# The last plain float32 product of a block-multiplied up projection, rewritten in three fp32r passes and dealt to other banks

## The chip, the cores and the metric

The kernel runs on one NeuronCore of one Trainium2 chip. The metric is the device time of one execution in microseconds, as the median of several runs. TensorE (PE) multiplies, VectorE (DVE), ScalarE (ACT) and GpSimd (POOL) work on vectors, and SyncE (SP) and GpSimd issue DMAs.

## The reference

One inference step of a one-layer decoder, all in float32, for 512 prompt tokens and 8 × 4 sample tokens (544 columns). The mixer in front is untouched. The part at hand is the convolutional feed-forward:

```python
u = h @ w_ffn_up                        # 1024 -> 2 x 2816: a gate half and a value half
ext = concatenate([conv_state, u], axis=1)
c = conv_b + sum(conv_w[i] * ext[:, i:i + T] for i in range(3))
g, val = c[..., :2816], c[..., 2816:]
f = (gelu(g) * val) @ w_ffn_down
```

## The kernel before

Activations lie transposed, features over the 128 partitions and the 544 tokens as columns. Each of the two halves of `u` has 22 tiles of 128 features. A float32 product is made as three passes in fp32r: weights and activations are each split into a high part (rounded by a copy on ScalarE) and a low part (the difference, on VectorE), and `high*high`, `high*low` and `low*high` are added up in a bank.

The first three pairs of tiles (gate tile n and value tile n) are multiplied plainly. From pair n = 3 (`NPLAIN`) to 21 a block scheme makes the four 2x2 blocks of (gate, value) x (tokens 0 to 271, tokens 272 to 543), each with 8 blocks of the contraction, from 7 products instead of 8. A product has 4 contraction blocks of 128 and 272 columns. Its weights are the gate weights (products 1 and 2), sums of weights "s13" (products 5 and 7) and "s24" (products 6 and 3), and, for product 4, the upper half of the value weights `v_high`. Its activations are halves of the hidden state (`T1h`, `T1l`) or the sums t1 to t4. Six products go in three fp32r passes (`three_passes`, lines 2245 to 2247, 12 matmuls each). Product 4 (line 2306) is 4 plain float32 matmuls on the raw `v_high` and `t4raw`; the profile records two matmuls for each.

TensorE's order for pair n, with what each waits for: 6 (s24 low part, `s1_ready`), 5, 7 (`q_ready`), 1 of pair n+1 (gate low part), 4 (`r_neg`), 3 (`u_two[1]`), 2 of pair n+1. Products 1, 6, 7 and 4 pile up in bank A, which ScalarE copies out after 1 (`keep_first`, line 1531), 6 (`keep_second`, 1537), 7 (`keep_third`, 1543) and 4 (`value_first`, 1550). Products 5 and 3 pile up in bank C, read on VectorE by `value_second` (2975 and 2976) and `gate_second` (2965 and 2966). Product 2 has bank 6 alone, read on VectorE by `gate_first` (2958).

The queues are written out by hand. In iteration n VectorE runs: `gate_second(n-1)`, `gate_first(n)`, the four taps of the convolution of pair n-1 (2849, 2855), `sum_2(n+1)` (2929), `sums_13_lo(n+1)` (2945), `value_second(n)`, `sum_4(n+1)` (2937), `f_product(n-1)` (2871), `gate_lo(n+2)` (2917), `sums_24_lo(n+1)` (2951). ScalarE runs: `first_tap(n-1, 0)` (1483), `keep_second(n)`, `sums_13_hi(n+1)` (1514), `keep_third(n)`, `gelu(n-1)` (1489), `gate_hi(n+2)` (1504), `keep_first(n+1)`, `sums_24_hi(n+1)` (1524), `value_first(n)`, `first_tap(n, 1)`.

SyncE loads the weights of later pairs: when product 2 of pair n is done the gate weights of pair n+2 (`load_g`, line 704, 512 KB), when product 7 is done the low value half of pair n+3 (711, 2 x 256 KB), when product 4 is done the high value half of pair n+2 (715, 256 KB), and right behind it one DMA that moves a piece of the attention cache from DRAM to DRAM (674, mostly 511 KB). GpSimd adds weights onto the landed low half by accumulating DMAs (993, 2 x 256 KB), and copies the heads and tails of the convolution (974, 983, 984).

After pair 21 comes the down projection (lines 1673 to 1675, sample tokens at 1692). Its operands `fTh` and `fTl` come from `f_high` (ScalarE) and `f_low` (VectorE), and those of the first four tiles are made while the last pair runs.

## Time and profile before

| What | Value |
|---|---|
| Time, median of 3 runs | 987.57 us (986.95 to 987.87) |
| The profiled execution's own time | 986.23 us |
| Its span, first to last instruction | 984.4 us |
| TensorE matmul busy | 960.6 us (98%) |
| VectorE, ScalarE, GpSimd busy | 600.7, 424.0, 276.2 us |
| Granted TensorE clock, mean | 0.999 |
| HBM traffic | 242 GB/s over the span |

The profile page splits the span by engine. Matmuls overlap (one starts before the one before it has drained), so the distance from start to start is what a matmul costs, not its duration. The trace can be asked for rows in order of time (start, length, engine, line, what is written and read, and in brackets the idle time ahead of it and what ended it), for groups by line, for waits, and for busy time in a stretch. The block scheme runs from about 628 to 838 us, the down projection behind it to the end.

### The profile page before, as it was taken

Reading aid. Unit: us, or ns where it says so; the run is one execution under the profiler, and the core shown is the slowest. Engines: PE = TensorE matmul, PEld = TensorE weight load, DVE = VectorE, ACT = ScalarE, POOL = GpSimd, SP = SyncE. Lnnn points to the kernel's source line nnn. Section 1 sums busy time; section 2 is a strip of 40 time slices with the busy share of each in tenths; the row PEclk is TensorE's granted clock in tenths of the full one; section 3 lists DMA queues with packets and bytes.
Section 4 is the critical chain, followed back from the end, with each engine's and each line's share of the span. In section 5 each row is a group of like instructions: output and inputs, shape, how many; then the busy total and the mean of one; then the engine's idle time right before and its main releaser. Section 6 shows DMA issues by size and latency. Waiting matters only on the chain. (4 is left out here: it accounts for less than half of the span.)

```text
span 984.4 us, 19132 instructions
## 1 busy us (share of the span) xinstructions
PE 960.6 (98%) x7470; PEld 845.5 (86%) x7470; DVE 600.7 (61%) x1030; ACT 424.0 (43%) x851; POOL 276.2 (28%) x412
## 2 busy tenths in 40 slices
PE   6999999999999999999999999999999999999997
PEld 4888787779999989999888788899999999777775
DVE  5455125436356887876127588798888888533235
ACT  5333323432543333333224366565566556433313
POOL 1102003144171344445201006235653650000200
PEclk9999999999999999999999999999999999999999
DMA  7534445555697677678834357678887882444853
GB/s 290 201 128 159 170 167 181 183 171 172 249 307 252 223 229 236 191 237 268 285 108 160 122 176 246 149 206 214 219 219 209 218 207 88 171 160 151 299 182 120
DMA packets 55750, 195.03 MB, mean 198 GB/s; under 512 B 8312, under 2 KB 14904, under 8 KB 54128
## 3 DMA queue, kind: packets, MB, share of 16 engines
q1 hardware_dynamic: 32336, 130.17, 39.0%
q0 software_dynamic: 23040, 63.07, 23.1%
q8 instruction: 59, 0.97, 0.4%
q10 hardware_dynamic: 288, 0.59, 0.2%
q14 instruction: 27, 0.22, 0.1%
HBM read 181.57 MB, written 56.27 MB: 242 GB/s over the span
## 5 line engine op out<-in xcount | busy, mean ns | idle before, releaser
L2370 DVE TENSOR_TENSOR wlo<-wraw,whi 128x1024 fp32r<-128x1024 f32 x94 | 114.8, 1221 | 258.9 <-ACT whi L1053 258.7
L1053 ACT ACTIVATE whi<-wraw 128x1024 fp32r<-128x1024 f32 x94 | 99.7, 1060 | 299.8 <-PE bank L1675 185.5
L1673 PE MATMUL bank<-whi,T1h 128*128 128x512 f32 (+1 forms) x288 | 113.5, 394 | 0.1
L1760 PE MATMUL bank<-T1h,whi 128*128 128x272 f32 x384 | 113.4, 295 | 0.0
L1766 PE MATMUL bank<-T1h,wlo 128*128 128x272 f32 x384 | 111.0, 289 | 0.0
L1765 PE MATMUL bank<-T1l,whi 128*128 128x272 f32 x384 | 110.4, 287 | 0.0
L1675 PE MATMUL bank<-whi,T1l 128*128 128x512 f32 (+1 forms) x288 | 109.9, 382 | 0.0
L1674 PE MATMUL bank<-wlo,T1h 128*128 128x512 f32 (+1 forms) x288 | 109.9, 381 | 0.0
L1760 PEld LDWEIGHTS bank<-T1h,whi 128*128 128x128 f32 x384 | 72.3, 188 | 4.8 <-issue 4.5
L1765 PEld LDWEIGHTS bank<-T1l,whi 128*128 128x128 f32 x384 | 72.4, 189 | 0.0
L1766 PEld LDWEIGHTS bank<-T1h,wlo 128*128 128x128 f32 x384 | 72.2, 188 | 0.0
L1673 PE MATMUL bank<-whi,fTh 128*128 128x512 f32 x176 | 71.4, 406 | 0.0
L1674 PE MATMUL bank<-wlo,fTh 128*128 128x512 f32 x176 | 69.5, 395 | 0.0
L1675 PE MATMUL bank<-whi,fTl 128*128 128x512 f32 x176 | 69.4, 394 | 0.0
L1673 PEld LDWEIGHTS bank<-whi,T1h 128*128 128x128 f32 x288 | 58.1, 202 | 12.7 <-issue 3.9
L1675 PEld LDWEIGHTS bank<-whi,T1l 128*128 128x128 f32 x288 | 58.1, 202 | 9.9
L1674 PEld LDWEIGHTS bank<-wlo,T1h 128*128 128x128 f32 x288 | 58.3, 202 | 8.8
L993 POOL DMA_DIRECT2D s_raw<-in_weights x38 | 37.5, 1209 | 77.6 <-DMA s_raw<-in_weights 77.5
L984 POOL COPY cv_tail<-u 128x16 f32<-128x16 f32 x44 | 54.2, 1569 | 0.0
L983 POOL COPY cv_tail<-u 128x2 f32<-128x2 f32 x44 | 43.5, 1241 | 27.1 <-ACT u L1550 22.4
L974 POOL COPY u<-cv_state 128x16 f32<-128x16 f32 x44 | 43.5, 1131 | 24.0 <-DVE c L2855 18.7
L2569 DVE TENSOR_TENSOR prod<-kvk,qbc 128x512 f32<-128x512 f32 x48 | 33.0, 687 | 23.7 <-DMA qbc<-sample_queries 22.8
(367 smaller groups left out, 2594.2 us busy)
## 6 DMA issues: line engine op xcount, KB each, us to landing
wraw<-in_weights SPq DMA_DIRECT2D x102, 512.0 KB, 4.4
out_s_kv_g<-in_cache_kv_g SPq DMA_DIRECT2D x64, 511.0 KB
qbc<-sample_queries POOLq DMA_DIRECT2D x48, 256.0 KB, 4.9
s_raw<-in_weights SPq DMA_DIRECT2D x38, 256.0 KB, 3.7
g_raw<-in_weights SPq DMA_DIRECT2D x19, 512.0 KB, 6.2
s_raw<-in_weights POOLq DMA_DIRECT2D x38, 256.0 KB, 7.1
kvk<-in_cache_kv_g POOLq DMA_DIRECT2D x32, 256.0 KB, 3.9
kvv<-in_cache_kv_g POOLq DMA_DIRECT2D x16, 512.0 KB, 8.4
```

Source lines behind the costliest of these rows:

```text
L974: nc.gpsimd.tensor_copy(u_samples(n, j)[:, :, 0:2], cvs[:, 16 * tile:16 * tile + 16].rearrange("p (b t) -> p b t", t=2)).then_inc(head_rea ...
L983: nc.gpsimd.tensor_copy(cvt[:, 18 * tile:18 * tile + 2], ubs[:, n % 3, j, SEQ:SEQ + 2])
L984: nc.gpsimd.tensor_copy(cvt[:, 18 * tile + 2:18 * tile + 18].rearrange("p (b t) -> p b t", t=2), u_samples(n, j)[:, :, 4:6]).then_inc(tail ...
L993: pool.dma_start(s13_raw[r][:, 2 * a_:2 * a_ + 2, :], src, accum_op=ALU.add).then_inc(sum_in[r], 16)
L1053: nc.scalar.activation(w_halves(s)[0], w_source(s), ACT.Copy).then_inc(w_hi, 1)
L1673: one = mm(P[i][:, 0:w], xh, Wh, start=st, stop=False)
L1674: mm(P[i][:, 0:w], xh, Wl, start=False, stop=False)
L1675: return one, mm(P[i][:, 0:w], xl, Wh, start=False, stop=sp_)
L1760: one = mm(dst, Wh, Th[:, k, c], start=k == 0, stop=False)
L1765: mm(dst, Wh, Tl[:, k, c], start=False, stop=False)
L1766: last = mm(dst, Wl, Th[:, k, c], start=False, stop=k == kt - 1)
L2370: v.tensor_tensor(lo, w_source(s), hi.bitcast(F), ALU.subtract).then_inc(w_lo, 1)
```

## The change

Product 4 goes through `three_passes` like the others. For that `v_high` is split on each pair by `value_hi` (ScalarE, 128x512) and `value_lo` (VectorE, 128x512), and t4 once by `operand_hi` and `operand_lo` (128x1088). The high part of `v_high` has a single buffer, so `value_hi(n)` waits for product 4 of the pair before. The high part of t4 lies where `fTl` of the first tiles is written later, so `f_low` of tiles 0 to 3 waits for the last product 4.

The products are dealt anew. Bank A gets 1, 6, 5, 3 and bank C gets 7, 4, and the order on TensorE is 6, 7, 5, 1 of n+1, 3, 4, 2 of n+1. So `keep_third` copies after product 5, `gate_second` moves to ScalarE (two copies out of bank A after product 3), and `value_first` moves to VectorE (after product 4). Wherever gate and value come in turn, the gate comes first: taps, GpSimd's heads and tails. On ScalarE `gelu(n-1)` goes ahead of `keep_third(n)`. Loads keep their rules, with the low value half now behind product 5 and the high value half still behind product 4, which is now the last but one in the order. The diff also renames semaphores (three into one, `s_soft`); those hunks, the `PRODUCT_NO[.., 7]` that become `[.., 5]` in ScalarE's waits, and the reorder ahead of the loop are left out below.

```diff
-        order += [(n, 6), (n, 5), (n, 7)] + [(n + 1, 1)] * nxt + [(n, 4), (n, 3)] + [(n + 1, 2)] * nxt
+        order += [(n, 6), (n, 7), (n, 5)] + [(n + 1, 1)] * nxt + [(n, 3), (n, 4)] + [(n + 1, 2)] * nxt
...
+    v_high_lo = [sb(f"v_high_lo{e}", VH_AT[e], [128, 512], R) for e in range(2)]
+    v_high_hi = sb("v_high_hi", 51752, [128, 512], R)
+    assert 51752 + 512 <= 52392
+    t4lo = sb("t4lo", TT0 + 6528, [128, 4, HALF], R)
+    t4hi = sb("t4hi", 4352, [128, 4, NTOK], R)[:, :, HALF:NTOK]
...
-        return 2 * n + 2 - j
+        return 2 * n + 1 + j
...
-            sp.wait_ge(product, PRODUCT_NO[n, 7])
+            sp.wait_ge(product, PRODUCT_NO[n, 5])
             if n + 3 < FT:
                 load_v_low(n + 3)
             sp.wait_ge(product, PRODUCT_NO[n, 4])
...
             act.wait_ge(t_raw, 2 + k)
+            if k == 4:
+                act.wait_ge(w_used, S_UP + 2 * NPLAIN)
             nc.scalar.activation(hi[:], raw[:], ACT.Copy).then_inc(t_hi, 1)
...
+        def value_hi(n):
+
+            e = pair_set(n)
+            act.wait_ge(vh_in[e], set_count(n))
+            if n > NPLAIN:
+                act.wait_ge(product, PRODUCT_NO[n - 1, 4])
+            nc.scalar.activation(v_high_hi[:], v_high[e][:], ACT.Copy).then_inc(vh_hi, 1)
+
...
-            act.wait_ge(product, PRODUCT_NO[n, 7])
+            act.wait_ge(product, PRODUCT_NO[n, 5])
             act.wait_ge(u_two[1], n)
-            nc.scalar.activation(rr[:], P[bank_a(n)][:, 0:HALF], ACT.Copy, scale=-1.0).then_inc(r_neg, 1)
-
-        def value_first(n):
-
-            act.wait_ge(product, PRODUCT_NO[n, 4])
-            act.wait_ge(conv_done, conv_no(n - 3, 1))
-            act.wait_ge(tail_done, conv_no(n - 3, 1))
-            nc.scalar.activation(ubs[:, n % 3, 1, 2:2 + HALF], P[bank_a(n)][:, 0:HALF], ACT.Copy, scale=-1.0).then_inc(u_one[1], 1)
+            nc.scalar.activation(rr[:], P[bank_a(n)][:, 0:HALF], ACT.Copy).then_inc(h_kept, 1)
+
+        def gate_second(n):
+
+            b = P[bank_a(n)]
+            act.wait_ge(product, PRODUCT_NO[n, 3])
+            act.wait_ge(conv_done, conv_no(n - 3, 0))
+            act.wait_ge(tail_done, conv_no(n - 3, 0))
+            nc.scalar.activation(ubs[:, n % 3, 0, 2 + HALF:2 + SEQ], b[:, 0:SEQ - HALF], ACT.Copy)
+            nc.scalar.activation(u_samples(n, 0)[:, :, 2:6], by_tokens(b[:, SEQ - HALF:HALF]), ACT.Copy).then_inc(u_two[0], 1)
...
         for n in range(NPLAIN, FT):
-            first_tap(n - 1, 0)
+            first_tap(n - 1, 1)
             keep_second(n)
+            if n == NPLAIN:
+                operand_hi(4, t4raw, t4hi)
+                value_hi(NPLAIN)
             if n + 1 < FT:
                 sums_13_hi(n + 1)
             else:
                 w_split(S_DN + 1)
                 f_high(2)
+            gelu(n - 1)
             keep_third(n)
-            gelu(n - 1)
...
-            value_first(n)
-            first_tap(n, 1)
-        first_tap(FT - 1, 0)
+            gate_second(n)
+            if n + 1 < FT:
+                value_hi(n + 1)
+            first_tap(n, 0)
+        first_tap(FT - 1, 1)
...
-        def product_5(n):
+        def product_7(n):
             e = pair_set(n)
             pe.wait_ge(s13_lo, pair_no(n))
-            pe.wait_ge(t_lo, 3)
             if n >= NPLAIN + 2:
-                pe.wait_ge(u_two[0], n - 1)
+                pe.wait_ge(u_one[1], n - 1)
             elif e:
                 pe.wait_ge(u_two[1], NPLAIN)
-            three_passes(P[bank_c(n)], True, *sums_13(n, 1), 0, lambda k: t1hi[:, k, :], lambda k: t1lo[:, k, :])
-
-        def product_7(n):
+            three_passes(P[bank_c(n)], True, *sums_13(n, 0), 0, lambda k: t3hi[:, k, :], lambda k: t3lo[:, k, :])
+
+        def product_5(n):
+
+            pe.wait_ge(q_ready, pair_no(n))
+            three_passes(P[bank_a(n)], False, *sums_13(n, 1), 0, lambda k: t1hi[:, k, :], lambda k: t1lo[:, k, :])
+
+        def product_4(n):
             e = pair_set(n)
-            pe.wait_ge(q_ready, pair_no(n))
-            three_passes(P[bank_a(n)], False, *sums_13(n, 0), 0, lambda k: t3hi[:, k, :], lambda k: t3lo[:, k, :])
-
-        def product_4(n):
+            pe.wait_ge(vh_lo, pair_no(n))
+            pe.wait_ge(t_lo, 4)
+            pe.wait_ge(u_two[1], n + 1)
+            three_passes(P[bank_c(n)], False, v_high_hi, v_high_lo[e], 0, lambda k: t4hi[:, k, :], lambda k: t4lo[:, k, :])
+
+        def product_3(n):
             e = pair_set(n)
-            pe.wait_ge(vh_in[e], set_count(n))
-            pe.wait_ge(t_raw, 6)
-            pe.wait_ge(r_neg, pair_no(n))
-            for k in range(4):
-                last = mm(P[bank_a(n)][:, 0:HALF], v_high[e][:, 128 * k:128 * k + 128], t4raw[:, k, :], start=False, stop=k == 3, skip_group_check=True)
-            last.then_inc(product, 1)
-
-        def product_3(n):
-
-            e = pair_set(n)
-            pe.wait_ge(u_two[1], n + 1)
-            three_passes(P[bank_c(n)], False, s24_high[e], s24_low[e], 512, lambda k: T1h[:, 4 + k, second_half], lambda k: T1l[:, 4 + k, second_half])
+            pe.wait_ge(h_kept, pair_no(n))
+            three_passes(P[bank_a(n)], False, s24_high[e], s24_low[e], 512, lambda k: T1h[:, 4 + k, second_half], lambda k: T1l[:, 4 + k, second_half])
         product_1(NPLAIN)
         product_2(NPLAIN)
         for n in range(NPLAIN, FT):
             product_6(n)
+            product_7(n)
             product_5(n)
-            product_7(n)
             if n + 1 < FT:
                 product_1(n + 1)
+            product_3(n)
             product_4(n)
-            product_3(n)
...
             dve.wait_ge(f_hi, n + 1)
+            if n < 4:
+                dve.wait_ge(product, PRODUCT_NO[FT - 1, 4])
...
+        def value_lo(n):
+
+            e = pair_set(n)
+            dve.wait_ge(vh_hi, pair_no(n))
+            dve.wait_ge(s24_made, 2 * pair_no(n) - 1)
+            v.tensor_tensor(v_high_lo[e][:], v_high[e][:], v_high_hi[:].bitcast(F), ALU.subtract).then_inc(vh_lo, 1)
...
-        def gate_second(n):
+        def value_first(n):
+
+            dve.wait_ge(product, PRODUCT_NO[n, 4])
+            dve.wait_ge(q_ready, pair_no(n))
+            v.scalar_tensor_tensor(ubs[:, n % 3, 1, 2:2 + HALF], P[bank_c(n)][:, 0:HALF], -1.0, qq[:], ALU.mult, ALU.subtract
+                                   ).then_inc(u_one[1], 1)
+
+        def value_second(n):
             b = P[bank_c(n)]
-            dve.wait_ge(product, PRODUCT_NO[n, 3])
-            dve.wait_ge(q_ready, pair_no(n))
-            v.tensor_tensor(ubs[:, n % 3, 0, 2 + HALF:2 + SEQ], b[:, 0:SEQ - HALF], qq[:, 0:SEQ - HALF], ALU.add)
-            v.tensor_tensor(u_samples(n, 0)[:, :, 2:6], by_tokens(b[:, SEQ - HALF:HALF]), by_tokens(qq[:, SEQ - HALF:HALF]), ALU.add
-                            ).then_inc(u_two[0], 1)
-
-        def value_second(n):
-
-            b = P[bank_c(n)]
-            dve.wait_ge(product, PRODUCT_NO[n, 5])
-            dve.wait_ge(r_neg, pair_no(n))
+            dve.wait_ge(product, PRODUCT_NO[n, 7])
+            dve.wait_ge(h_kept, pair_no(n))
             dve.wait_ge(tail_done, conv_no(n - 3, 1))
-            v.tensor_tensor(ubs[:, n % 3, 1, 2 + HALF:2 + SEQ], rr[:, 0:SEQ - HALF], b[:, 0:SEQ - HALF], ALU.subtract)
-            v.tensor_tensor(u_samples(n, 1)[:, :, 2:6], by_tokens(rr[:, SEQ - HALF:HALF]), by_tokens(b[:, SEQ - HALF:HALF]), ALU.subtract
-                            ).then_inc(u_two[1], 1)
+            v.scalar_tensor_tensor(ubs[:, n % 3, 1, 2 + HALF:2 + SEQ], b[:, 0:SEQ - HALF], -1.0, rr[:, 0:SEQ - HALF], ALU.mult, ALU.subtract)
+            v.scalar_tensor_tensor(u_samples(n, 1)[:, :, 2:6], by_tokens(b[:, SEQ - HALF:HALF]), -1.0, by_tokens(rr[:, SEQ - HALF:HALF]),
+                                   ALU.mult, ALU.subtract).then_inc(u_two[1], 1)
...
-                gate_second(n - 1)
+                value_first(n - 1)
             gate_first(n)
             conv(n - 1)
+            if n == NPLAIN:
+                operand_lo(4, t4raw, t4hi, t4lo)
+            value_lo(n)
             if n + 1 < FT:
                 sum_2(n + 1)
                 sums_13_lo(n + 1)
-            else:
-                f_low(0)
-                f_low(1)
             value_second(n)
...
-                f_low(2)
-                f_low(3)
-        gate_second(FT - 1)
+                for k in range(4):
+                    f_low(k)
+        value_first(FT - 1)
```

## Rows read from the trace of the kernel before

**Rows 1.** The page, first part: busy time, share, instructions.

```profile
PE 960.6 (98%) x7470; PEld 845.5 (86%) x7470; DVE 600.7 (61%) x1030; ACT 424.0 (43%) x851; POOL 276.2 (28%) x412
```

**Rows 2.** Busy time of the engines over 15 pairs, granted clock, DMA share.

```profile
643.76:807.35 163.59, 163.48 (x1202) 158.51 (x1202) 144.06 (x226) 99.78 (x151) 85.73 (x122) 1.00 0.84 214
```

**Rows 3.** Groups by line and shape, 600 to 860 us: busy, mean ns.

```profile
L2306 PE MATMUL bank<-t4raw,v_high 128*128 128x272 f32 x152 | 38.1, 393 | 1.9 <-ACT rr L1543 1.9
...
L2929 DVE TENSOR_TENSOR s_raw<-s_raw,v_high 128x512 f32<-128x512 f32 x19 | 13.0, 683 | 3.7 <-DMA s_raw<-in_weights 3.7
...
L2905 DVE SCALAR_TENSOR_TENSOR t4raw<-t2raw,x_sum 128x1088 f32<-128x1088 f32 x1 | 1.3, 1291 | 0.0
```

**Rows 4.** Timeline of TensorE through one pair: start, length, line.

```profile
730.66 0.28 PE L2245 MATMUL bank<-t2hi,s_high 128*128 128x272 f32 x1
...
735.16 0.29 PE L2245 MATMUL bank<-T1h,g_high 128*128 128x272 f32 x1
...
736.68 1.99 PE L2306 MATMUL bank<-t4raw,v_high 128*128 128x272 f32 x8
738.31 0.49 PE L2245 MATMUL bank<-T1h,s_high 128*128 128x272 f32 x1
738.63 0.29 PE L2246 MATMUL bank<-T1l,s_high 128*128 128x272 f32 x1
...
741.53 0.29 PE L2245 MATMUL bank<-t2hi,s_high 128*128 128x272 f32 x1
```

**Rows 5.** Timeline of VectorE through one pair that waited for nothing.

```profile
709.14 0.44 DVE L2958 TENSOR_TENSOR u<-bank,s 128x272 f32<-128x272 f32 x1 [0.73 <-PE bank L2247]
709.50 1.50 DVE L2849 SCALAR_TENSOR_TENSOR c<-u,convp,c 128x560 f32<-128x560 f32 x2
...
717.08 1.22 DVE L2951 TENSOR_TENSOR s_low<-s_raw,s_high 128x1024 fp32r<-128x1024 f32 x1
```

**Rows 6.** Timeline of all engines around one late load of gate weights.

```profile
738.70 0.33 SPq L715 DMA_DIRECT2D v_high<-in_weights  x1
739.07 0.52 SPq L674 DMA_DIRECT2D out_s_kv_g<-in_cache_kv_g  x1
...
740.05 1.77 POOL L993 DMA_DIRECT2D s_raw<-in_weights  x2 [3.93 <-DMA s_raw<-in_weights]
...
741.73 0.33 SPq L704 DMA_DIRECT2D g_raw<-in_weights  x1
...
746.53 0.66 ACT L1489 ACTIVATE c<-c 128x560 f32<-128x560 f32 x1
749.07 1.06 ACT L1504 ACTIVATE g_high<-g_raw 128x1024 fp32r<-128x1024 f32 x1 [1.88 <-DMA g_raw<-in_weights]
...
751.40 1.22 DVE L2951 TENSOR_TENSOR s_low<-s_raw,s_high 128x1024 fp32r<-128x1024 f32 x1
...
752.68 0.39 PE L2245 MATMUL bank<-t2hi,s_high 128*128 128x272 f32 x1
```

**Rows 7.** Waits between 640 and 820 us: total, times, longest.

```profile
ACT g_high L1504 <- DMA g_raw<-in_weights: 12.7, 11, 1.9
```

**Rows 8.** Timeline of ScalarE: the two other latest gate loads.

```profile
650.82 1.06 ACT L1504 ACTIVATE g_high<-g_raw 128x1024 fp32r<-128x1024 f32 x1 [1.57 <-DMA g_raw<-in_weights]
...
814.62 1.06 ACT L1504 ACTIVATE g_high<-g_raw 128x1024 fp32r<-128x1024 f32 x1 [1.81 <-DMA g_raw<-in_weights]
```

**Rows 9.** DMA share in 40 slices of 0.15 us, 738 to 744 us.

```profile
DMA  9984111100099369992999990002735996596567
```

**Rows 10.** Timeline at the first pair and behind the last one.

```profile
637.18 1.06 ACT L1514 ACTIVATE s_high<-s_raw 128x1024 fp32r<-128x1024 f32 x1 [3.99 <-DMA s_raw<-in_weights]
...
638.67 2.07 PE L2306 MATMUL bank<-t4raw,v_high 128*128 128x272 f32 x8 [1.36 <-ACT rr L1543]
...
838.35 1.08 PE L1692 MATMUL bank<-wraw,fTs 128*32 128x128 f32 x32 [0.30 <-PE bank L2247]
...
839.36 0.50 PE L1673 MATMUL bank<-whi,fTh 128*128 128x512 f32 x1
```

More of the change, by code:

```diff
@@ L512, in build_layer @@
     kw_in = [sem(f"kw_in{e}") for e in range(2)]
-    s_step, pads_ready, qbd_ready, v_used, s_probs = (sem("s_step"), sem("pads_ready"), sem("qbd_ready"),
-                                                     sem("v_used"), sem("s_probs"))
-    s_max, s_exp, o_row, os_hi, os_lo = (sem(n) for n in ("s_max", "s_exp", "o_row", "os_hi", "os_lo"))
+    s_step, pads_ready, qbd_ready, v_used, s_soft = (sem("s_step"), sem("pads_ready"), sem("qbd_ready"),
+                                                     sem("v_used"), sem("s_soft"))
+    o_row, os_hi, os_lo = (sem(n) for n in ("o_row", "os_hi", "os_lo"))
     branch_done = sem("branch_done")
@@ L526, in build_layer @@
     vl_in, sum_in = ([sem(f"{nm_}{e}") for e in range(3)] for nm_ in ("vl_in", "sum_in"))
-    g_hi, g_lo, s13_hi, s13_lo, s24_made, s24_hi, s24_lo = (
-        sem(nm_) for nm_ in ("g_hi", "g_lo", "s13_hi", "s13_lo", "s24_made", "s24_hi", "s24_lo"))
+    g_hi, g_lo, s13_hi, s13_lo, s24_made, s24_hi, s24_lo, vh_hi, vh_lo = (
+        sem(nm_) for nm_ in ("g_hi", "g_lo", "s13_hi", "s13_lo", "s24_made", "s24_hi", "s24_lo", "vh_hi", "vh_lo"))
     t_raw, t_hi, t_lo = sem("t_raw"), sem("t_hi"), sem("t_lo")
-    s1_ready, q_ready, r_neg = sem("s1_ready"), sem("q_ready"), sem("r_neg")
+    s1_ready, q_ready, h_kept = sem("s1_ready"), sem("q_ready"), sem("h_kept")
     x2_moved = sem("x2_moved")
@@ L968, in conv_heads @@
         def conv_heads(n):
-            for j in (1, 0):
+            for j in (0, 1):
                 tile = n + FT * j
@@ L977, in conv_tails @@
         def conv_tails(n):
-            for j in (1, 0):
+            for j in (0, 1):
                 tile = n + FT * j
@@ L1046, in w_split @@
             elif s == S_DN:
-                act.wait_ge(product, PRODUCT_NO[FT - 2, 7])
+                act.wait_ge(product, PRODUCT_NO[FT - 2, 5])
                 assert sum_set(FT - 3) == 1
@@ L1510, in sums_13_hi @@
             if n >= NPLAIN + 2:
-                act.wait_ge(product, PRODUCT_NO[n - 2, 7])
+                act.wait_ge(product, PRODUCT_NO[n - 2, 5])
             elif e:
@@ L1570, in _ @@
         w_split(S_UP + 3)
+        first_tap(0, 0)
         first_tap(0, 1)
-        first_tap(0, 0)
         operand_hi(1, t3raw, t3hi)
@@ L1582, in _ @@
         sums_13_hi(3)
+        first_tap(1, 0)
         first_tap(1, 1)
-        first_tap(1, 0)
         columns(2, 0)
@@ L1587, in _ @@
         gelu(1)
+        first_tap(2, 0)
         columns(2, 1)
-        first_tap(2, 1)
         keep_first(3)
@@ L1606, in _ @@
             else:
-                act.wait_ge(product, PRODUCT_NO[FT - 2, 7])
+                act.wait_ge(product, PRODUCT_NO[FT - 2, 5])
                 if n == FT - 2:
@@ L1996, in sample_turn @@
         def sample_turn():
-            pe.wait_ge(s_probs, 1)
+            pe.wait_ge(s_soft, 3)
             turn(("sp",), [srow[:, g, 0:128] for g in range(NG)], 128)
@@ L2261, in product_1 @@
             if n >= NPLAIN + 2:
-                pe.wait_ge(u_one[1], n - 1)
+                pe.wait_ge(u_two[0], n - 1)
             elif e:
@@ L2858, in conv @@
         def conv(n):
+            second_tap(n, 0)
             second_tap(n, 1)
-            second_tap(n, 0)
+            third_tap(n, 0)
             third_tap(n, 1)
-            third_tap(n, 0)
         def f_product(n):
```

18 lines of the change are left out of this document (9 added, 9 removed).

## The prediction

> **What bounds the kernel now.** I read the page first: matmuls fill 98% of the span [rows 1]. Then the stretch of 15 pairs from one gate load to the fifteenth after it: 163.59 us, so 10.91 us a pair. TensorE is busy in 163.48 of it at full clock, VectorE in 144.06 (9.60 a pair), ScalarE in 99.78 (6.65) [rows 2]. So TensorE sets the pace here, and VectorE is the next in line with 1.3 us to spare. The groups and TensorE's timeline then say what a product costs [rows 3, 4], VectorE's timeline how long its chain is [rows 5], and the rows around a late load what happens when weights come late [rows 6 to 8]: that is the one other thing that reaches TensorE in this stretch.
>
> **Product 4 itself.** Products 6, 5 and 7 take from 730.66 to 735.16: 1.50 us each, 125 ns a matmul. The float32 product starts at 736.68, the next one at 738.31, and that one's second matmul comes 0.32 later instead of 0.125. So product 4 costs 1.63 + 0.195 = 1.825 us [rows 4]. In three passes it is a product like the others, same shape and same kind of operands: 1.50. Gain 0.325 a pair, times 19 pairs: 6.2 us. The pair's period without waits goes from 10.87 (730.66 to 741.53) to about 10.53.
>
> The Trainium skill (FP8 and Floating Point Precision, TensorE Precision Notes) says that true float32 takes four passes through the array. By that the product would be 16 passes against 12 and each pair would gain 0.50, 9.5 us in all. The trace puts it at 1.825 us, 14.6 passes of 125 ns, and the trace decides.
>
> **VectorE.** With no wait, its chain from `gate_first` to the end of `sums_24_lo` takes 709.14 to 718.30, 9.16 us [rows 5]. The change adds `value_lo`, 0.68 long and about 0.60 from start to start, since neighbours overlap by some 0.08 [rows 3]. `gate_second` goes, and `value_first` comes in its place in front of `gate_first`, as long as `gate_first`, 0.36 from start to start (709.14 to 709.50) [rows 5]. Subtractions become scalar_tensor_tensor with an immediate, whose row (1291 ns for 1088 columns) shows no markedly dearer rate than 683 ns for 512 [rows 3]; I count 0.02. The cycle is then 9.16 - 0.08 + 0.60 + 0.36 + 0.02 = 10.06 us against 10.53. Priced from below at nothing for the new form and from above at 0.1 for each of the three, it stays between 10.04 and 10.36: hidden, with 0.2 to 0.5 to spare. If that cover were gone, each 0.1 over would cost 1.8 us over 18 pairs.
>
> **ScalarE.** It gains `value_hi` (1024 columns take 1.06 [rows 10], so 512 about 0.6) and two copies for one; 6.65 becomes some 7.5 of 10.53, hidden. `value_hi(n+1)` waits for product 4 of n, which ends 9.2 us into the pair, and holds up only `first_tap(n, 0)` behind it, which then ends about at the start of the next pair; VectorE reads it 0.6 us later. Two gaps that look alarming are thus covered. `gelu` goes ahead of `keep_third`, but it ends before product 5 does, so it delays nothing in a steady pair.
>
> **First and last pair.** In pair 3 ScalarE sits until 637.18 for a DMA of weight sums, and TensorE waits at 638.67 for the copy behind it [rows 10]. That DMA doesn't move. `gelu(2)` now stands between, 0.56 from start to start, then t4's and `v_high`'s low parts (1.2 and 0.6) lengthen VectorE's queue, and pair 4 starts later by 0.2 where it should have started 0.3 earlier: cost 0.5. At the end, `f_low(0)` and `f_low(1)`, like 683 ns for 512 columns [rows 3] and so 0.7 each, were hidden and now wait for the last product, while the sample matmuls cover only 1.0 us (838.35 to 839.36) [rows 10] and some of the hand-over: cost 0.3. The convolution of pair 21 is pushed back by the four `f_low`, some 2.8 us, but its result is needed only many weight slots later. Nothing else of the down projection changes.
>
> **Gate loads: the term that decides.** The chain for pair n+2's gate weights is load, `gate_hi`, `keep_first`, `sums_24_hi`, `sums_24_lo`, then product 6. In the late case the load is issued at 741.73 and `gate_hi` starts at 749.07, 7.34 after. `sums_24_lo` ends at 752.62, 3.55 later, and product 6 starts at 752.68 instead of 752.40 [rows 6]. The issue stands 0.2 behind the start of product 6. So a load costs nothing as long as `gate_hi` starts within 10.87 - 0.2 - 3.55 = 7.1 us of it now, and within 6.78 with the shorter pair. `gate_hi` waited for the load in 11 pairs, 12.7 us in all [rows 7]; it begins to wait about 5.46 after the issue (746.53 + 0.66 - 741.73) [rows 6]. Waits over 1.32 cross the new limit: 1.57, 1.88 and 1.81 [rows 6, 8], so 0.25 + 0.56 + 0.49 = 1.3 us of stalls. About 0.5 of this is in the time before already (752.68 against 752.40, and the third alike). Net cost with loads as they are: 0.8.
>
> But loads don't stay as they are. The high value half and the cache move behind it are issued after product 4. Now this is 3.0 us before the gate load (738.70 and 739.07 against 741.73) [rows 6]. With product 4 last but one, only product 2 lies between: 1.5 us. The two keep the DMA engines full from about 739.65 to 741.6. Then comes a gap of 0.45, and from 742.05 on the accumulating DMAs (issued at 740.05) and the gate load share the engines [rows 6, 9]. Shifted by 1.5, they reach 1.0 us into that shared stretch. Bounds for the delay of the gate load: 1.0 if all of the overlap is passed on. At the other end it is below nothing, because the low halves are issued at the same place of a pair that is 0.33 shorter, so the accumulating DMAs reach the engines that much later against the gate load; -0.3. The shared stretch has slices at 2 to 7 tenths [rows 9], room that takes up much of the overlap, so I take +0.25.
>
> The Trainium skill (DMA: Bandwidth & Descriptors, Queues, rings and completion order) says that a DMA engine takes turns between its queues packet by packet and finishes one before it switches. That speaks against the change, since the cache move is the DMA with the biggest pieces, and a gate load would wait behind one; it is the mechanism of the third rival below.
>
> A stall falls behind product 2, so the next load is already issued, and a pair pays only what is over 6.78 less the stall before it. Going through the delays of the 16 loads from 643.76 to 807.35 in order (the three longest stand in [rows 6, 8]), stalls come to 1.3 us with no shift, 2.4 with +0.25, 3.7 with +0.5, 5.4 with +0.75 and 7.2 with +1.0.
>
> **Sum.** -6.2 + 0.5 + 0.3 - 0.5 (stalls of before that go) = -5.9 without load stalls; with those at +0.25, -3.5 us. The sum is made on the profiled execution, 986.23 us with a span of 984.4; the median of the runs shown, 987.57, is 1.3 above it, and I apply the difference there: 984.0 us.
>
> **Rivals.** First, the full gain: gate loads never reach TensorE, perhaps because the later accumulating DMAs give them room. For it: `gate_hi` waited for its load in 11 pairs only [rows 7]. Time: 987.6 - 5.9 = 981.7. Second, no change to speak of: the load slips by 0.55 to 1.1, and stalls of 3.9 to 7.9 eat the gain; 985.6 to 989.6. For it: the engines are 84% busy [rows 2]. Against: the gaps in [rows 9]. Third, the other side: the move's big pieces stand in front of every gate load, and it slips by more than 1.1. The gain is gone from +0.8 on, and each further 0.25 costs 1.7 us; at +1.35 stalls come to 9.6, and the time to 991.3. Place: product 6 of each pair waiting for `sums_24_lo`. Fourth, VectorE becomes the bound, from a cycle of 10.53 on; to lose the whole gain it would need 10.85, 0.8 over my sum, which no row supports. It would show as TensorE waiting though `gate_hi` never waits; 984 to 988.
>
> **How the numbers follow.** 0.2% (2 us) is about what a measurement of this kernel can tell from no change. Chances: the forecast (2 to 5 faster) 0.50; the full gain 0.15; no change 0.19; slower by more than 2 through late loads 0.13; VectorE 0.03, counted for the most part with no change. Faster 0.65, same 0.21, slower 0.14. The range goes from the full gain, 981.6, to 988.8, a little past break-even; some 0.13 lie above it and 0.05 below. The forecast's own range is 982.6 to 985.6.
>
> **What would show it.** Matmuls of line 2306 gone, 12 in their place with starts 125 ns apart and no 0.32 gap behind. Gate loads 10.5 to 10.7 us apart instead of 10.91. VectorE near 10.1 busy of each pair. High value half and move issued 1.5 us before the gate load. TensorE's waits, if any, at product 6 for `sums_24_lo`, in the pairs in which `gate_hi` waited more than 1.3 for its load. The prediction is wrong if the start to start of `gate_hi` after its load rises by more than 0.7 on average, if VectorE's cycle exceeds 10.5, or if product 4 in three passes is slower than its neighbours.

## The result, and the profile after

| | Before | After |
|---|---|---|
| Median, 8 runs each, same chip | 987.88 us (986.39 to 989.37) | 990.16 us (988.86 to 991.66) |
| Ratio, 95% interval | | 1.0027 [1.0016, 1.0039] |
| Span of the profiled execution | 984.4 us | 987.1 us |
| TensorE clock, mean | 0.999 | 0.997 |

The change made the kernel slower by 0.27%. The forecast was 984.0 us, in a range of 981.6 to 988.8.

The page of the kernel after, first part, answers to [rows 1]:

```profile
PE 957.6 (97%) x7546; PEld 847.5 (86%) x7546; DVE 611.4 (62%) x1031; ACT 434.1 (44%) x890; POOL 281.2 (28%) x412
```

TensorE is busy for 3 us less in a span 2.7 us longer, so it waits more. The windows view says where. Its columns are the window, its length, busy time of PE, PEld, DVE, ACT and POOL, the granted clock, the DMA share and GB/s. The first two windows are the first pair, the third is the stretch from the gate load of pair 5 to the fifteenth after it, which answers to [rows 2]:

```profile
636.00:639.00 3.00, 0.00 (x0) 0.00 (x0) 1.82 (x3) 1.90 (x4) 0.59 (x2) 1.00 1.19 224
639.00:642.70 3.70, 3.65 (x17) 3.65 (x18) 3.70 (x7) 2.75 (x6) 1.11 (x3) 0.55 0.32 103
645.41:811.00 165.59, 160.83 (x1263) 158.77 (x1262) 151.45 (x226) 106.08 (x181) 86.79 (x115) 1.00 0.80 213
```

A pair takes 11.04 us instead of 10.91, and TensorE is idle for 4.8 us of the stretch where it was idle for 0.1. That is one loss. The other is in the first pair: TensorE stands still for the whole of 636 to 639, and then goes at a granted clock of 0.55. The kernel before has full clock in the same window:

```profile
639.00:642.70 3.70, 3.70 (x26) 3.43 (x25) 3.70 (x7) 3.44 (x6) 1.18 (x3) 1.00 0.63 205
```

Product 4 itself is as cheap as forecast. On TensorE's timeline it runs from 739.94 to 741.44, 1.50 us, and its neighbour product 3 from 738.43 to 739.94 as well. Compare 1.825 in [rows 4]:

```profile
738.43 0.29 PE L2267 MATMUL bank<-T1h,s_high 128*128 128x272 f32 x1
...
739.94 0.29 PE L2267 MATMUL bank<-t4hi,v_high_hi 128*128 128x272 f32 x1
...
741.44 0.29 PE L2267 MATMUL bank<-T1h,g_high 128*128 128x272 f32 x1
```

The waits between 640 and 820 us answer to [rows 7]. The last line, TensorE's own waits, is new, and the weight loads' line above it had 0.6 us in 2 waits before:

```profile
ACT g_high L1511 <- DMA g_raw<-in_weights: 30.9, 15, 3.8
...
DVE g_low L2937 <- ACT g_high L1511: 10.6, 11, 2.4
PEld bank L2267 <- DVE s_low L2978: 6.5, 8, 2.0
PE bank L2267 <- DVE s_low L2978: 4.6, 4, 1.8
```

The chain of one late load, all engines in order of time, answers to [rows 6]:

```profile
708.69 0.33 SPq L720 DMA_DIRECT2D v_high<-in_weights  x1
709.06 0.52 SPq L679 DMA_DIRECT2D out_s_kv_g<-in_cache_kv_g  x1
710.19 0.63 SPq L709 DMA_DIRECT2D g_raw<-in_weights  x1
...
718.16 1.06 ACT L1511 ACTIVATE g_high<-g_raw 128x1024 fp32r<-128x1024 f32 x1 [2.91 <-DMA g_raw<-in_weights]
...
719.25 1.23 DVE L2937 TENSOR_TENSOR g_low<-g_raw,g_high 128x1024 fp32r<-128x1024 f32 x1 [1.54 <-ACT g_high L1511]
720.49 1.23 DVE L2978 TENSOR_TENSOR s_low<-s_raw,s_high 128x1024 fp32r<-128x1024 f32 x1
...
721.76 0.39 PE L2267 MATMUL bank<-t2hi,s_high 128*128 128x272 f32 x1 [0.92 <-DVE s_low L2978]
```

The high value half and the cache move are issued 1.50 and 1.13 us ahead of the gate load, as the prediction said. But `gate_hi` starts 7.97 us after the issue, and not some 0.25 later than before. The list of DMA issues between 640 and 830 us gives the gate load (x16, KB each, median us to landing) 7.0 us, where the same list of the kernel before has 6.3. After, then before:

```profile
g_raw<-in_weights SPq DMA_DIRECT2D x16, 512.0 KB, 7.0
```

```profile
g_raw<-in_weights SPq DMA_DIRECT2D x16, 512.0 KB, 6.3
```

The first pair on ScalarE and TensorE answers to [rows 10]:

```profile
637.10 1.06 ACT L1521 ACTIVATE s_high<-s_raw 128x1024 fp32r<-128x1024 f32 x1 [3.96 <-DMA s_raw<-in_weights]
638.07 0.65 ACT L1494 ACTIVATE c<-c 128x560 f32<-128x560 f32 x1
638.62 0.38 ACT L1558 ACTIVATE rr<-bank 128x272 f32<-128x272 f32 x1
...
639.05 0.39 PE L2267 MATMUL bank<-T1h,s_high 128*128 128x272 f32 x1 [3.33 <-ACT rr L1558]
...
639.90 0.43 PE L2268 MATMUL bank<-T1l,s_high 128*128 128x272 f32 x1
640.13 0.43 PE L2269 MATMUL bank<-T1h,s_low 128*128 128x272 f32 x1
```

ScalarE waits for the same DMA as before and `keep_third` stands behind it. TensorE's idle time is 3.33 us instead of 1.36, mostly since it had come to that point 1.6 us sooner (635.72 against 637.31), and the matmuls behind it start 0.23 us apart instead of 0.125, which is the lower of the clock's two levels, 1.2 GHz.

**The account by stretches**, all from the profiled executions. The gate load of pair 5 is issued 1.65 us later than before (645.41 against 643.76). The 15 pairs take 2.0 us more (165.59 against 163.59). From the last gate load to the end it is 0.95 less (987.1 - 811.00 = 176.1 against 984.4 - 807.35 = 177.05). Together +2.7, the difference of the spans. These are single executions; what an edit in a stretch is worth is read from the medians below as well.

### The profile page after: what moved, and what is told of

It reads as the page before. It is cut to its first block and busy times, and to the rows that moved or that the text cites. A ratio compares the mean times of both kernels' runs of the same rounds, so it can differ in the third digit from the quotient of the medians.

```text
span 987.1 us, 19365 instructions
## 1 busy us (share of the span) xinstructions
PE 957.6 (97%) x7546; PEld 847.5 (86%) x7546; DVE 611.4 (62%) x1031; ACT 434.1 (44%) x890; POOL 281.2 (28%) x412
## 5 line engine op out<-in xcount | busy, mean ns | idle before, releaser
L988 POOL COPY cv_tail<-u 128x2 f32<-128x2 f32 x44 | 49.0, 1242 | 27.8 <-ACT u L1567 20.6
L979 POOL COPY u<-cv_state 128x16 f32<-128x16 f32 x44 | 47.4, 1288 | 29.4 <-DVE c L2873 23.9
L989 POOL COPY cv_tail<-u 128x16 f32<-128x16 f32 x44 | 51.6, 1363 | 0.0
```

Of the source, the lines that this page charges most:

```text
L989: nc.gpsimd.tensor_copy(cvt[:, 18 * tile + 2:18 * tile + 18].rearrange("p (b t) -> p b t", t=2), u_samples(n, j)[:, :, 4:6]).then_inc(tail ...
```

## The experiments

Theory A blames the order of issue ahead of the gate load, theory B the shorter pair alone, theory C the first pair. Times are medians of 6 to 12 runs, and ratios are to the kernel before in the same session, whose median was 987.84 us for experiments 1 to 4, 988.15 for 5 to 8, 988.96 for 9 to 11 and 987.57 for 12. So a difference between two experiments of different sessions is given by times and by ratios where the two disagree.

**Experiment 1: three passes alone.** Product 4 in three passes, but banks, order and queues of before, with the loads of `v_high` and the cache move 3.0 and 2.6 us ahead of the gate load. Core of the edit to the kernel before:

```diff
         def product_4(n):
-            for k in range(4):
-                last = mm(P[bank_a(n)][:, 0:HALF], v_high[e][:, 128 * k:128 * k + 128], t4raw[:, k, :], start=False, stop=k == 3, skip_group_check=True)
-            last.then_inc(product, 1)
+            three_passes(P[bank_a(n)], False, v_high_hi, v_high_lo[e], 0, lambda k: t4hi[:, k, :], lambda k: t4lo[:, k, :])
```

> Product 4 in three passes, but banks and order of products as in the kernel before, so that the high value half and the cache move stay 3.0 us ahead of the gate load. Theory A (these two, issued 1.5 us later, delay the gate load): gate_hi waits for its load about as in the kernel before, 12 to 18 us in all, the loads follow each other every 10.6 to 10.7 us, and the time is 984 to 986.5 against 987.9 before. Theory B (a shorter pair alone makes the loads late, whatever the order): gate_hi waits 25 us or more, pairs of 10.9 to 11.0, 987 to 989. Theory C (at the first pair TensorE idles 3.3 us and then runs at the lower clock; 1.6 us): here product 4 of pair 3 follows the same copy as before, so the idle time stays under 3 us and the granted clock at 1.00 or nearly so.

Measured 982.91 us, ratio 0.9958 [0.9943, 0.9973]. The 15 pairs take 160.56 us, 10.70 each:

```profile
643.27:803.83 160.56, 159.48 (x1262) 158.71 (x1263) 153.11 (x243) 105.30 (x166) 86.62 (x119) 1.00 0.85 218
```

So the shorter product is worth 4.9 us where nothing else moves. `gate_hi` waits 15.2 us in all for its loads, as theory A has it, though the time is 1.1 us below theory A's range. Theory B falls. In the first pair TensorE is idle for 1.95 us and the granted clock stays at 1.00, as theory C expected.

**Experiment 2: the move goes elsewhere.** The kernel after, with the cache move issued behind the low value half.

```diff
                 load_v_low(n + 3)
+            move(*next(moves))
             sp.wait_ge(product, PRODUCT_NO[n, 4])
             load_v_high(n + 2)
-            move(*next(moves))
```

> The changed kernel, with the cache move issued behind the low value half instead of behind the high one. Theory A: the gate load lands earlier, gate_hi waits 12 to 20 us instead of 30.9, and the time falls by 2 to 4 us to 986 to 988. Theory B: no change, 989.5 to 991. Theory C says nothing of it: the first pair is untouched and keeps its lower clock from 639 to 643.

Measured 984.09 us, ratio 0.9960 [0.9946, 0.9973]: 6.1 us less than the kernel after, more than expected. TensorE is idle for 0.3 us in the 15 pairs, which take 10.63 us each, and the gate load's median landing is 6.0 us:

```profile
646.79:806.27 159.48, 159.22 (x1262) 158.31 (x1261) 150.74 (x225) 106.81 (x181) 93.77 (x116) 1.00 0.86 217
```

The high value half still stands 1.5 us ahead of the gate load here, and no harm from it by itself is seen. The first pair keeps its loss.

**Experiment 3: no move in the loop.** The kernel after, with all moves of the loop issued among the weight loads of the down projection.

```diff
             load_v_high(n + 2)
-            move(*next(moves))
...
-            for m in itertools.islice(moves, 1 if s % 10 else 2):
+            for m in itertools.islice(moves, 2):
```

> The changed kernel, with no cache move in the block scheme at all: all of them go in the down projection, two behind each weight slot. Theory A: as with the move behind the low half or better, loads every 10.55 to 10.65 us, 985.5 to 987.5. Theory B (the load on the DMA engines per pair is the matter): about the same gain as A says, but none with the move behind the low half. If the down projection can't hide them, the last stretch grows from its present length.

Measured 985.38 us, ratio 0.9976 [0.9964, 0.9987]. The pairs are the tightest yet, 158.68 / 15 = 10.58 us. Yet the total is worse than in experiment 2, as the stretch behind the last gate load takes 178.3 us instead of 176.1. TensorE waits there, once, for weights; that the two moves behind each load make them late is likely, not shown:

```profile
935.45 0.65 PE L1713 MATMUL bank<-wraw,fTs 128*32 128x128 f32 x16 [1.83 <-DMA wraw<-in_weights]
```

**Experiment 4: the first pair's queues.** The kernel after; in pair 3 alone ScalarE runs `gelu` and `keep_third` ahead of `sums_13_hi(4)`, and `gate_hi(5)` after `sums_24_hi(4)`; VectorE runs `value_second(3)` ahead of `sum_2(4)`, and both `sums_.._lo(4)` ahead of `gate_lo(5)`.

```diff
+            if n == NPLAIN:
+                gelu(n - 1)
+                keep_third(n)
+                sums_13_hi(n + 1)
-            if n + 1 < FT:
+            elif n + 1 < FT:
                 sums_13_hi(n + 1)
```

> The changed kernel, with the queues of the first pair alone put in another order: ScalarE copies product 5 out before it waits for pair 4's weight sums, VectorE runs value_second(3) ahead of sum_2(4) and makes pair 4's s24 first. Theory C: TensorE idles 1 us or less in front of product 3 of pair 3, the clock stays at 1.00, and the first gate load of the loop comes 3 to 4 us earlier; 986.5 to 987.5. Rival: pair 4's weight sums by DMA set the start anyway, the idle time moves to product 6 of pair 4 with the same loss of clock, and the gain is under 1 us: 989 to 990.

Measured 987.02 us, ratio 0.9990 [0.9979, 1.0001], 3.1 us less than the kernel after. The two windows of the first pair, below, show no long idle stretch and no lower clock. The first gate load is issued at 640.83, 4.6 us earlier, but the gain isn't kept whole: the second follows 12.61 us later (10.54 in the kernel after), and the 15 pairs take 168.17 us, 2.6 more than there.

```profile
636.00:639.00 3.00, 3.00 (x26) 3.00 (x25) 2.20 (x6) 1.04 (x2) 0.97 (x2) 1.00 1.10 182
639.00:642.70 3.70, 2.71 (x22) 2.49 (x21) 3.70 (x5) 3.59 (x8) 0.10 (x1) 1.00 1.26 391
```

**Experiment 5: the suspected place in the kernel before.** Only the move is issued later; the high value half stays.

```diff
             load_v_high(n + 2)
+            sp.wait_ge(product, PRODUCT_NO[n, 3])
             move(*next(moves))
```

> The kernel before, with one edit: in each pair the cache move is issued after product 3 instead of after product 4, so some 1.1 us ahead of the next gate load, as in the kernel after, and not 2.6 us ahead of it. Product 4 stays in plain float32 and the banks and their order stay. Theory A (the cache move just ahead of the gate load delays that load by 0.8 to 0.9 us, and the stall of TensorE comes from there): gate_hi begins 7.0 to 7.3 us after the issue instead of 6.4, which passes the limit of this longer pair in some 8 of 15 pairs, so +2 to +5 us, 990 to 993 us. Rival B (the late load costs only because the pair became shorter; in the old pair the slack of 0.33 us and the waits of before absorb it): +0 to +1 us, 988 to 989 us.

Measured 989.60 us, ratio 1.0015 [1.0005, 1.0025], +1.4 us: between the two theories (+2 to +5, and 0 to +1). The move stands 1.5 us ahead of the gate load here, not the 1.1 of the expectation, which it has in the kernel after only because the high value half is issued first. The median landing of the gate load goes from 6.3 to 6.7 us, less than the 7.0 of the kernel after.

**Experiment 6: the new order alone.** The kernel after, with product 4 as four plain float32 matmuls in bank C and without the parts that split its operands.

```diff
         def product_4(n):
-            three_passes(P[bank_c(n)], False, v_high_hi, v_high_lo[e], 0, lambda k: t4hi[:, k, :], lambda k: t4lo[:, k, :])
+            for k in range(4):
+                last = mm(P[bank_c(n)][:, 0:HALF], v_high[e][:, 128 * k:128 * k + 128], t4raw[:, k, :], start=False, stop=k == 3, skip_group_check=True)
+            last.then_inc(product, 1)
```

> The kernel after with product 4 in four plain float32 matmuls again, as before: the new banks and the new order alone. Theory A and C (the order costs by the move ahead of the gate load and by the first pair, and does so whatever product 4 is): first pair +1.6 us, pairs of 10.87 us plus the stalls of late loads of +1 to +4 us, so 990 to 993.5 us. Rival B (the order is harmless, the shorter pair alone meets the late loads): 987.5 to 989 us, that of before plus the first pair at most.

Measured 993.88 us, ratio 1.0061 [1.0045, 1.0077]. The order alone costs 5.7 us, with gate loads landing after 7.3 us (median). So the change is the sum of a gain and a loss: -4.9 (experiment 1) and +5.7, which would be +0.8; together they are +2.3. That a late load weighs more on a shorter pair may explain the 1.5 us between, but the intervals of the three ratios are as wide as that.

**Experiment 7: TensorE kept busy.** The kernel after with 24 extra matmuls, once, in the idle stretch of the first pair, into a bank that is opened anew afterwards.

```diff
+            if n == NPLAIN:
+                pe.wait_ge(u_two[1], NPLAIN)
+                for k in range(24):
+                    mm(P[bank_c(n + 1)][:, 0:HALF], T1h[:, k % 4, 0:128], T1h[:, k % 4, first_half], start=True, stop=True)
             pe.wait_ge(h_kept, pair_no(n))
```

> The kernel after with 24 extra matmuls (3.0 us) once, in the first pair between product 1 of pair 4 and product 3 of pair 3, into the bank that product 7 of pair 4 will open anew: work that nothing reads, in the 3.3 us in which TensorE was idle. Nothing that is waited for comes earlier by it. Theory C (the idle costs twice, once as the wait and once more by the lower granted clock behind it): the granted clock stays at 1.00 through the next 4 us, the 15 matmuls at 228 ns go at 125 ns, and the time falls by 1.2 to 1.6 us, to 988.5 to 989 us. Rival (the lower clock is only seen, the next wait takes up what it cost): no change within 0.3 us, 989.9 to 990.4 us. A second rival (the clock falls for another reason than the idle): the granted clock is 0.5 to 0.6 in that stretch all the same.

Measured 988.16 us, ratio 1.0002 [0.9991, 1.0013], 2.0 us less than the kernel after, with 3 us of work more. The windows:

```profile
636.00:639.00 3.00, 2.85 (x24) 2.63 (x22) 1.64 (x4) 1.46 (x2) 0.84 (x2) 1.00 1.19 216
639.00:642.70 3.70, 3.20 (x25) 3.20 (x26) 3.70 (x7) 3.09 (x7) 0.57 (x2) 1.00 0.45 133
```

Product 3 started no sooner (639.50 against 639.05), and still the next gate load was issued 1.1 us earlier (644.33 against 645.41), so the same work took 1.5 us less. The idle time brought the lower clock, and the lower clock cost real time. Net of the later start, the first pair gains 1.1 us; the rest of the 2.0 lies in the 15 pairs (164.44 against 165.59 us), which the edit doesn't touch, and is no more than executions scatter.

**Experiment 8: both repairs.** The edits of experiments 2 and 4 in the kernel after.

```diff
+            move(*next(moves))
             sp.wait_ge(product, PRODUCT_NO[n, 4])
...
+            if n == NPLAIN:
+                gelu(n - 1)
+                keep_third(n)
+                sums_13_hi(n + 1)
```

> The kernel after with both repairs: the cache move issued behind the low value half, and the queues of ScalarE and VectorE in the first pair in the order that lets keep_third go ahead of the wait for the sums of pair 4. Theory A and C as two separate losses: the two gains add up, -6.1 and -3.1 us from 990.2, so 980.5 to 982.5 us, with pairs of 10.6 us and the clock at 1.00 in the first pair. Rival (they overlap, the later pairs take up what the first pair loses): no better than the better of the two, 983.5 to 984.5 us.

Measured 979.75 us, ratio 0.9919 [0.9906, 0.9933]. It is the fastest of all, 8.4 us under the kernel before. The gains add up as two separate losses should (-6.1 and -3.1 from 990.2 would be 981.0, 1.2 more than measured; by the ratios, -0.67% and -0.37% from 1.0027, it would be 0.9923). The first pair behind the first gate load takes 11.98 us. From the second gate load on, 14 pairs take 148.05 us, 10.58 each, with TensorE idle for 0.1 us:

```profile
653.64:801.69 148.05, 147.93 (x1178) 147.88 (x1179) 140.78 (x212) 100.22 (x169) 86.92 (x113) 1.00 0.89 221
```

**Experiment 9: the move's place in the old order.** Experiment 1 with the edit of experiment 5.

```diff
             load_v_high(n + 2)
+            sp.wait_ge(product, PRODUCT_NO[n, 3])
             move(*next(moves))
```

> Experiment 1 (three passes of product 4 in the banks and the order of before, 982.9 us) with one edit: the cache move is issued after product 3, some 1.1 us ahead of the gate load, and not after product 4. Theory A (the place of the move in SP's queue is the loss, and it costs more the shorter the pair is: in the longer pair it cost 1.5 us over before): +3 to +6 us, 986 to 989 us, with gate_hi 7.0 to 7.4 us after the issue. Rival (the new order carries the loss in its product and bank waits and the move alone does little): +0 to +1.5 us, 983 to 984.5 us.

Measured 984.34 us, ratio 0.9960 [0.9943, 0.9977]. That is +1.4 by the times and +0.2 by the ratios, both the rival's number. The move alone, moved close to where the kernel after has it (1.5 us ahead of the gate load, not 1.1), doesn't explain the loss; theory A as first put falls here.

**Experiment 10: the first pair in the old order.** Experiment 1 with the first pair's queues reordered as in experiment 4, `keep_third` ahead of `gelu`.

```diff
+            if n == NPLAIN:
+                keep_third(n)
+                gelu(n - 1)
+                sums_13_hi(n + 1)
```

> Experiment 1 with the queues of ScalarE and VectorE in the first pair reordered as in experiment 4: keep_third goes ahead of the wait for the sums of pair 4. Theory C (TensorE's idle of 1.95 us behind that wait goes, and as the clock did not fall in experiment 1 nothing more): -1 to -2 us, 981 to 982 us. Rival (the sums of pair 4 set the pace anyway, the idle moves to product 6 of pair 4): within 0.5 us of 982.9.

Measured 982.94 us, ratio 0.9940 [0.9920, 0.9959]. By the times this is no gain over experiment 1, as the rival has it; by the ratios it is 1.8 us (0.9940 against 0.9958), as theory C has it, since the kernel before measured 1.1 us more beside it than beside experiment 1. The intervals cover both, so the median doesn't decide. In the profiled execution the first pair did get shorter: from `keep_second(3)` to product 4 it is 639.15 - 633.81 = 5.34 us against 638.35 - 631.90 = 6.45, and TensorE's idle time there falls from 1.95 to 0.83 us. From `keep_second(3)` to the second gate load it is 21.10 us against 22.41, 1.3 less, so this one execution shows theory C's gain. This execution came to the pair 1.9 us later, ahead of the edit, and its other 14 pairs took 1.3 us more (150.82 against 149.52), which together hide the gain in the span.

**Experiment 11: both repairs in the old order.** Experiment 10 with the move of experiment 2.

```diff
+            move(*next(moves))
             sp.wait_ge(product, PRODUCT_NO[n, 4])
             load_v_high(n + 2)
-            move(*next(moves))
```

> Experiment 1 with both repairs, the first pair's queues and the cache move behind the low value half: the counterpart of experiment 8 in the order of before. In experiment 1 the pairs are 10.70 us apart against 10.56 to 10.58 us with the move out of the way, so beyond the first pair -0 to -2 us: 979.5 to 981.5 us, level with experiment 8. Rival (the new order is better in itself once its two losses are gone): above experiment 8 by over 1 us.

Measured 979.94 us, ratio 0.9912 [0.9892, 0.9931], 3.0 us less than experiment 10 in the same session and level with experiment 8. Without its two losses the new order is neither better nor worse than the old.

**Experiment 12: both DMAs at the suspected place.** Experiment 1 with the high value half and the move both issued where the kernel after issues them.

```diff
-            sp.wait_ge(product, PRODUCT_NO[n, 4])
+            sp.wait_ge(product, PRODUCT_NO[n, 3])
             load_v_high(n + 2)
             move(*next(moves))
```

> Experiment 1 again, and now both the load of the value tile's high half and the cache move are issued after product 3, 1.5 and 1.1 us ahead of the gate load, exactly where the kernel after has them; the banks and the order stay those of before. The move alone at that place cost 1.4 us (experiment 9), the high half alone at that place costs little if anything (experiment 2 has it there, with the move out of the way). Theory A as it now stands (the two together delay the gate load by most of a microsecond, and the loss is more than that of either alone): +3.5 to +6 us over experiment 1, 986.5 to 989 us, with gate_hi 7.0 us or more after the issue. Rival (the rest of the loss is of the new order itself, of its banks and of what waits for what): 984 to 985.5 us, as in experiment 9.

Measured 987.76 us, ratio 1.0002 [0.9993, 1.0011]: +4.9 us over experiment 1 (+4.3 by the ratios), with the banks and the order of products untouched, and the gate loads landing after 7.3 us (median). SyncE's issues of one pair, in experiment 9 and here:

```profile
706.02 0.33 SPq L720 DMA_DIRECT2D v_high<-in_weights  x1
707.53 0.52 SPq L679 DMA_DIRECT2D out_s_kv_g<-in_cache_kv_g  x1
709.04 0.75 SPq L709 DMA_DIRECT2D g_raw<-in_weights  x1
```

```profile
698.85 0.34 SPq L720 DMA_DIRECT2D v_high<-in_weights  x1
699.23 0.52 SPq L679 DMA_DIRECT2D out_s_kv_g<-in_cache_kv_g  x1
700.36 0.34 SPq L709 DMA_DIRECT2D g_raw<-in_weights  x1
```

This settles where the greater loss comes from: 256 KB and some 511 KB issued together, 1.5 and 1.1 us ahead of the gate load. The pieces in one table (pair: from gate load to gate load; landing: median of the gate loads in 640 to 830 us):

| Kernel | High half and move ahead of gate load | Pair | Landing | Its execution | Median time | Ratio |
|---|---|---|---|---|---|---|
| Experiment 2 | 1.5 us; behind the low half | 10.63 | 6.0 | 984.30 | 984.09 | 0.9960 |
| Experiment 1 | 3.0 and 2.6 us | 10.70 | 6.5 | 981.37 | 982.91 | 0.9958 |
| Experiment 9 | 3.0 and 1.5 us | 10.79 | 6.7 | 983.50 | 984.34 | 0.9960 |
| After | 1.5 and 1.1 us | 11.04 | 7.0 | 988.86 | 990.16 | 1.0027 |
| Experiment 12 | 1.5 and 1.1 us | 11.20 | 7.3 | 991.93 | 987.76 | 1.0002 |

Pair and landing are of one profiled execution, whose own time is in the fifth column. That of experiment 12 was the slowest of its twelve and that of the kernel after the fastest of its eight, so the step from one to the other in the third column isn't to be read as a difference of the kernels. The time of experiment 2 holds the loss of the first pair, those of experiments 1, 9 and 12 don't.

## Why the prediction was wrong

**Right.** Product 4: 1.50 us, and experiment 1 shows the gain, 4.9 of the 6.2 us; of the rest 1.0 us is TensorE's waits for `sums_24_lo` in its trace. VectorE: 151.45 / 15 = 10.10 us a pair against the 10.06 forecast. ScalarE: 106.08 / 15 = 7.07 (7.5 forecast), never in the way of a steady pair. The pair's own length: 10.53 forecast, 10.58 in experiments 3 and 8. The issue of high half and move 1.5 us ahead of the gate load, and TensorE's waits at product 6 for `sums_24_lo`. The end: 0.95 us shorter, 0.7 by my terms (three products 4 at -0.325, and +0.3 for `f_low`). The table of stalls, too, as the next paragraph shows. Of the rivals the second describes the gate loads (a slip of 0.55 to 1.1, stalls of 3.9 to 7.9 us). The time is in the third rival's band, slower by more than 2 us, only because the first pair's loss came on top; its place, product 6 waiting for `sums_24_lo`, was right.

**Wrong, first step: "so I take +0.25"** for the slip of the gate load. From the issue to the start of `gate_hi` it was 6.28 us in the mean of the 16 loads and is 7.24, so the slip is 0.96 (0.7 in the median landing). The prediction had named a rise of more than 0.7 as a sign of being wrong. What it made of a slip held: its table gives 5.4 us of stalls at +0.75 and 7.2 at +1.0, so 6.9 at +0.96, and its limit of 6.78 us, applied to the 16 measured delays in order, gives 6.4. The 15 pairs lost 165.59 - 15 x 10.53 = 7.6 us, of which 0.7 is that a pair without waits takes 10.58 and not 10.53. The worst load was issued at 753.96 and had `gate_hi` start 9.06 later:

```profile
763.02 1.06 ACT L1511 ACTIVATE g_high<-g_raw 128x1024 fp32r<-128x1024 f32 x1 [3.77 <-DMA g_raw<-in_weights]
```

I had bounds of -0.3 and 1.0 and chose near the low end, because slices at 2 to 7 tenths looked like room [rows 9]. The slip came out close to the upper bound, that of all the overlap passed on. A mean over 16 DMA engines doesn't tell whether one of them still has a piece of the move.

The trace's DMA records show the overlap itself. A move of 511 KB goes as 16 packets of 32,704 bytes, most of 1.3 to 1.9 us each, and a gate load as 128 packets of 4096 bytes. Counted from the issue of the gate load (medians), the last packet of the move ended at 1.7 us before and 1.9 in experiment 1, at 2.8 in experiment 9, at 3.9 in the kernel after and in experiment 12, and at 0.0 in experiment 2. The last packet of the gate load ended at 5.9, 6.2, 6.3, 6.6, 6.9 and 5.5 in the same order. In the kernel after its first packet started at 2.8, so some engines had begun on the gate weights while others were still at the move.

The Trainium skill (DMA: Bandwidth & Descriptors, Queues, rings and completion order) says that a DMA engine takes turns between its queues and finishes a packet before it turns to another. I had tied the third rival to that rule, and it isn't what lies between the move and the gate load here, as both stand on one queue. In the kernel after, between 640 and 830 us, the 30.16 MB of queue 1 match what SyncE issues, gate loads and moves included, and the 8.39 MB of queue 0 are GpSimd's accumulating DMAs:

```profile
q1 hardware_dynamic: 11221, 30.16, 49.6%
q0 software_dynamic: 5891, 8.39, 27.2%
```

The runs show the time that the place of issue costs, and that both DMAs are needed for it (experiments 2, 9, 12). Whether the rule delays a gate load behind the accumulating DMAs, no run here shows. How the overlap becomes a delay isn't shown either: the records don't name the engine of a packet, and the accumulating DMAs landed later as well (median 7.8 us against 6.9).

**Wrong, second step: "cost 0.5"** for the first pair, a sum that had no term for TensorE's clock. I forecast its end 0.2 us later and it came 1.65 later. TensorE reaches the wait 1.6 us sooner while the DMA that ends the wait doesn't move, and with `gelu` in between the release is 0.4 us later (639.05 against 638.67), so its idle time grows from 1.36 to 3.33 us. Part of the 1.6 is chance, as executions of kernels with the same queues come to this pair up to 2.3 us apart; but the idle time is 3.05 to 3.44 us in the four kernels that have the new queues unaltered in this pair, and 1.36 to 2.17 in the five that have the old ones so. The longer rest alone costs nothing, as the release is what counts. But behind it the granted clock was 0.55 over 3.7 us: 15 matmuls 0.1 us too slow, 1.5 us. Experiment 7 takes this away by itself, 1.5 us by its trace. Without it the forecast of 0.2 would have held.

**The sum again.** Over the three stretches my terms give +0.2, -3.2 and -0.7, so -3.7 us (-3.5 in the prediction; the difference is rounding of a pair's length); measured +1.65, +2.0 and -0.95, so +2.7. Of the difference of 6.4 us the gate loads are 5.2 and the first pair 1.45.

**Open.** Why the high half adds so much to the move (4.9 us together, 0.2 to 1.4 for the move alone, none seen for the half alone) isn't told apart further, nor what the move's 0.4 us less distance adds in experiment 12. No run moved the high half alone with the cache move left at 2.6 us.

## What to carry to other kernels

When an instruction is moved past a semaphore, list every DMA that is issued behind that semaphore and what is issued next on the same queue; here the arithmetic gained 4.9 us and two DMAs in a bad place lost 5. Price a later landing over its whole range (here stalls of 1.3 to 7.2 us) before choosing a point in it, and don't read spare room from the mean share of the DMA engines. Compare runs of two sessions by their ratios to a common kernel as well as by their times. Where TensorE has to wait a few microseconds in any case, look at the clock behind the wait, and give it something harmless to multiply or shorten the wait.

## What the runs showed of the hardware

TensorE's clock fell to its lower level behind single waits in kernels in which it is busy for 97% of the span. Idle times in the first pair of 3.05, 3.30, 3.33 and 3.44 us (experiments 6 and 3, the kernel after, experiment 2) were followed by a granted clock of 0.50 to 0.54 over 3.25, 3.49, 3.70 and 5.66 us; those of 1.36 (before), 1.95, 1.99, 2.02 and 2.17 us (experiments 1, 5, 12 and 9) were not. The length of the wait isn't all of it: in a steady pair of experiment 12 an idle time of 2.11 us was followed by 3 us at 0.50 to 0.53, seen in the starts of the matmuls and in the windows:

```profile
789.54 0.59 PE L2265 MATMUL bank<-t2hi,s_high 128*128 128x272 f32 x1 [2.11 <-DVE s_low L2978]
789.93 0.43 PE L2266 MATMUL bank<-t2lo,s_high 128*128 128x272 f32 x1
790.16 0.43 PE L2267 MATMUL bank<-t2hi,s_low 128*128 128x272 f32 x1
```

```profile
790.00:791.50 1.50, 1.50 (x8) 1.50 (x8) 1.50 (x3) 0.85 (x1) 0.32 (x2) 0.50 0.68 187
791.50:793.00 1.50, 1.50 (x8) 1.50 (x8) 1.50 (x3) 0.34 (x2) 0.55 (x1) 0.53 1.02 244
```

And a plain float32 product of 4 x 128x272 costs 1.825 us where three fp32r passes over the same operands cost 1.50.
